# A two-block transformer kernel: the opening in another order, the bias on ScalarE's DMA queue, the compression woven into a slab, normalising ahead of splits, and high parts first in the stages behind a norm

## The reference

```python
def first_block(x, ...):
    for i in range(2):
        hn = rms_norm(x, norm_mix[i])
        x = x + (even_mixer if i == 0 else odd_mixer)(hn, ...)
        x = x + jnp.square(jax.nn.relu(rms_norm(x, norm_mlp[i]) @ mlp_w1[i])) @ mlp_w2[i]   # 1024 -> 4096 -> 1024
    return rms_norm(x, norm_final)

def even_mixer(hn, w_in, w_out, ...):       # 8 heads in three branches, and 4 heads of differential attention
    q, kc, vc, ks, vs, kw, vw, g, dq, dk, dv = split(hn @ w_in)
    kc = compress_kv(kc, pos_k, w1_k, w2_k)  # 15 blocks of 32 tokens: gelu((block + pos) @ w1) @ w2
    vc = compress_kv(vc, pos_v, w1_v, w2_v)
    gates = sigmoid(g)                       # 3 gates per head, one per branch
    # softmax(q k' / 8 + bias[relative position]) v, for each branch and for the differential heads
    return concat([o_a, o_b]) @ w_out

def odd_mixer(hn, w_in, w_out, bias): ...    # 16 heads, q k v = hn @ w_in

def second_block(x, ...):                    # one layer
    # h @ w_in: a gated linear recurrence behind a short convolution, 16 heads of forgetting attention,
    # two gated projections, w_out, a norm and the residual; then w_up (1024 -> 6144), a short
    # convolution, gelu(gate) * value, w_down, a norm and the residual
```

## Time and profile before

| what | us |
|---|---|
| median of three runs | 1252.53 |
| lowest and highest of them | 1247.95, 1256.39 |
| the profiled execution, a run of its own | 1244.96 |
| its span in the profile | 1243.2 |

### The profile page before, as it was taken

The page is one execution under the profiler, slowest core; times in us unless marked ns, Lnnn a source line. Parts: engine busy times, 40 slices in busy tenths (PEclk is TensorE's granted clock), DMA queues, the critical chain, the costliest instruction groups (busy, mean ns, idle before and its releaser), DMA issues.

```text
span 1243.2 us, 21636 instructions
## 1 busy us (share of the span) xinstructions
PE 1158.9 (93%) x9407; PEld 1116.4 (90%) x9407; DVE 796.4 (64%) x1131; ACT 586.6 (47%) x823; POOL 147.4 (12%) x83
## 2 busy tenths in 40 slices
PE   6799888999999999999999999999977979999997
PEld 5798668999999899999999999999975879999997
DVE  6436546877454665787654788776554677888852
ACT  4146654443334464444433556654344446666531
POOL 3000004000031000400022202400060021110100
PEclk8879889999999999999999999999988998999999
DMA  8934205555555443656555371654951353656550
GB/s 218 221 101 136 69 2 162 177 187 187 188 186 169 136 137 106 200 179 194 181 192 178 121 206 41 197 158 150 318 189 35 103 169 105 201 173 218 177 195 36
DMA packets 198771, 195.71 MB, mean 157 GB/s; under 512 B 9692, under 2 KB 196757, under 8 KB 198677
## 3 DMA queue, kind: packets, MB, share of 16 engines
q1 hardware_dynamic: 194116, 190.72, 49.2%
q10 hardware_dynamic: 4560, 3.62, 1.0%
HBM read 192.86 MB, written 1.46 MB: 156 GB/s over the span
## 4 chain that ended last, share of the span: by engine, by line
PE 77%; DVE 9%; SPq 5%; DMA 3%; POOL 2%; ACT 1%; issue 1%; DVEq 0%; ACTq 0%; POOLq 0%
PE ps_gemm L1561 67%; PE ps_score L1626 2%; PE ps_out L1653 2%; DVE w_lo L1026 2%; PE ps_trans L1638 2%; PE ps_score L1837 2%; DMA f_bias<-cum_scr 2%; DVE prob L1066 1%; SPq L509 1%; PE ps_gemm L1731 1%; POOL f_bias L657 1%; SPq L553 1%; DVE act_lo L1032 1%; DMA raw<-in_w_in 1%; DVE prob L1095 1%
## 5 line engine op out<-in xcount | busy, mean ns | idle before, releaser
L1561 PE MATMUL ps_gemm<-act_hi,w_hi 128*128 128x256 f32 x1640 | 467.3, 285 | 27.0 <-DVE act_lo L1032 21.2
L1561 PE MATMUL ps_gemm<-act_lo,w_hi 128*128 128x256 f32 x1640 | 461.8, 282 | 0.0
L1561 PE MATMUL ps_gemm<-act_hi,w_lo 128*128 128x256 f32 x1640 | 461.5, 281 | 0.0
L1026 DVE TENSOR_TENSOR w_lo<-raw,w_hi 128x2048 fp32r<-128x2048 f32 (+2 forms) x179 | 409.5, 2295 | 69.1 <-ACT w_hi L698 68.7
L698 ACT ACTIVATE w_hi<-raw 128x2048 fp32r<-128x2048 f32 (+2 forms) x179 | 332.7, 1862 | 204.0 <-DMA raw<-in_mlp_w 97.9
L1561 PEld LDWEIGHTS ps_gemm<-act_hi,w_hi 128*128 128x128 f32 x1640 | 311.6, 190 | 35.8 <-issue 30.4
L1561 PEld LDWEIGHTS ps_gemm<-act_lo,w_hi 128*128 128x128 f32 x1640 | 311.6, 190 | 0.3
L1561 PEld LDWEIGHTS ps_gemm<-act_hi,w_lo 128*128 128x128 f32 x1640 | 311.3, 190 | 0.2
L1561 PE MATMUL ps_gemm<-hid_hi,w_hi 128*128 128x256 f32 x512 | 143.1, 280 | 0.0
L1561 PE MATMUL ps_gemm<-hid_hi,w_lo 128*128 128x256 f32 x512 | 143.1, 279 | 0.0
L1561 PE MATMUL ps_gemm<-hid_lo,w_hi 128*128 128x256 f32 x512 | 142.8, 279 | 0.0
(11 more groups left out here) (282 smaller groups left out, 1738.1 us busy)
## 6 DMA issues: line engine op xcount, KB each, us to landing
raw<-in_mlp_w SPq DMA_DIRECT2D x64, 1024.0 KB, 5.4
raw<-in_w_in SPq DMA_DIRECT2D x30, 1024.0 KB, 5.7
raw<-in_w_up SPq DMA_DIRECT2D x24, 1024.0 KB, 5.2
raw<-in_od_w_in SPq DMA_DIRECT2D x12, 1024.0 KB, 5.1
raw<-in_w_down SPq DMA_DIRECT2D x12, 1024.0 KB, 5.2
raw<-in_ev_w_in SPq DMA_DIRECT2D x9, 1024.0 KB, 8.4
raw<-in_w_proj_a SPq DMA_DIRECT2D x8, 640.0 KB, 4.3
raw<-in_ev_w_out SPq DMA_DIRECT2D x4, 1024.0 KB, 5.3
```

The costliest lines, as they stand in the source:

```text
L1026: dve.tensor_tensor(w_lo[:, slot, 0:k, 0:n], raw[:, slot, 0:k, 0:n], w_hi[:, slot, 0:k, 0:n].bitcast(F32), ALU.subtract).then_inc(w_ready, 1)
L1561: ins = pe.matmul(dst, lhs, rhs, start=(first and opens and i == 0 and half == 0 and q == 0), stop=(last and closes and i == len(ks) - 1 a ...
```

## The change

1. **DMA queues in the opening.** The 8 bias loads go from SyncE's queue to ScalarE's, with the wait for `brow_out` ahead of them. SyncE issues `cw1` directly behind the parameter rows, ahead of GATE and SV.
2. **ScalarE's order.** Split of slab 0, split of x, the write of the bias rows to HBM, split of slab 1, the wait, the 8 bias loads, `root(0)`, split of slab 2.
3. **TensorE's and VectorE's order.** The bias rows are made and copied behind the transposes and copies of x. The transposes of the parameter rows and their copies go behind Q0.
4. **Compression woven into SV.** `compress_chunk(k)` issues 8 of the 64 matmuls behind each of SV's 8 chunks. The wait for GATE's result to be moved out is in the first of them.
5. **VectorE in attention.** `normalise(i - 1)` goes ahead of the split of the low part.
6. **High parts first.** The first slab of each of the six stages behind a norm runs its 32 matmuls with x_hi, each chunk behind a wait for `act_hi`, and then its 16 matmuls with x_lo behind waits for `act_lo`.

No arithmetic is added or left out, only the order of the additions changes.

```diff
@@ SyncE @@
+        for i, name in enumerate(("k", "v")):
+            sp.dma_start(cw1[:, i, :, :], ...).then_inc(ld["cw"], 16)
         a_slab(GATE)
         a_slab(SV)
-        sp.wait_ge(brow_out, 16)
-        for a in range(P // 16):
-            sp.dma_start(nb[16 * a:16 * a + 16, :, :], src).then_inc(nb_in, 16)
-        for i, name in enumerate(("k", "v")):
-            sp.dma_start(cw1[:, i, :, :], ...).then_inc(ld["cw"], 16)
@@ ScalarE @@
+        split_hi(0)
+        act.wait_ge(par_ok, 1)
+        split_x(0)
         act.wait_ge(brow_ok, 1)
         act.dma_start(... scr_w ..., brow ...).then_inc(brow_out, 16)
-        split_hi(0)
-        act.wait_ge(par_ok, 1)
-        split_x(0)
-        for s in range(1, AHEAD):
-            split_hi(s)
+        split_hi(1)
+        act.wait_ge(brow_out, 16)
+        for a in range(P // 16):
+            act.dma_start(nb[16 * a:16 * a + 16, :, :], src).then_inc(nb_in, 16)
         root(0)
+        split_hi(2)
@@ VectorE, attention @@
+                if 1 <= i < n + 1:
+                    normalise(i - 1)
                 for part in FILL[p].get(i, ()):
                     if part[0] == "in":
                         in_slab(part[1], part[2] == 0, False)
-                if 1 <= i < n + 1:
-                    normalise(i - 1)
@@ VectorE, opening @@
-        dve.wait_ge(brow_ps, 1)
-        dve.tensor_copy(brow[:, :], ps_o[0:16, 0, 0:REL]).then_inc(brow_ok, 1)
...
         for gi in range(4):
             dve.wait_ge(xt, gi + 1)
             dve.tensor_copy(x[:, 2 * gi:2 * gi + 2, :], pair(gi)).then_inc(emptied[gi % 2], 1)
+        dve.wait_ge(brow_ps, 1)
+        dve.tensor_copy(brow[:, :], ps_o[0:16, 0, 0:REL]).then_inc(brow_ok, 1)
...
         a_slab(KV_CMP)
+        a_slab(Q0)
         dve.wait_ge(par_t, 2)
...
-        for j in range(Q0, DQ0):
+        for j in range(SKW, DQ0):
             a_slab(j)
@@ TensorE, gemm @@
+            order = [(k, half, q) for k in ks for half in halves for q in range(3)]
+            if low_last:
+                order = [(k, half, q) for qs in ((0, 2), (1,)) for k in ks for half in halves for q in qs]
+            for i, (k, half, q) in enumerate(order):
+                if before_chunk is not None and half == 0 and q < 2:
+                    before_chunk(k, q)
...
+                if between is not None and half == len(halves) - 1 and q == 2:
+                    between(k)
...
         def x_in(n):
-            def wait(c):
-                pe.wait_ge(xl, PRE_I[n] * NX + c + 1)
+            def wait(c, low):
+                pe.wait_ge(xl if low else xh, PRE_I[n] * NX + c + 1)
@@ TensorE, opening @@
-        pe.wait_ge(ld["bias"], 32)
-        pe.matmul(ps_o[0:16, 0, 0:REL], btab[:, :], buck[:, :], ...).then_inc(brow_ps, 1)
         pe.wait_ge(ld["x"], 32)
...
+        pe.wait_ge(ld["bias"], 32)
+        pe.matmul(ps_o[0:16, 0, 0:REL], btab[:, :], buck[:, :], ...).then_inc(brow_ps, 1)
...
+        def compress_chunk(k):
+            g = g0 + CMP1_GROUP
+            b = g % 2
+            if k == 0:
+                pe.wait_ge(emptied[b], gwait(g))
+                pe.wait_ge(ld["cw"], 16 * 6)
+                gi = g0 + A_GROUPS[KV_CMP]
+                pe.wait_ge(emptied[gi % 2], out_count(gi))
+            for m in range(4 * (k % 4), 4 * (k % 4) + 4):
+                i = k // 4
+                ins = pe.matmul(ps_g[:, b, ...], cw1[:, i, m, :], cmp2[:, i, :, ...], start=(m == 0), stop=(m == 15))
+            if k == KS - 1:
+                ins.then_inc(cmp_ps, 1)
...
         a_slab(0)
         stat(0)
+        a_slab(1)
+        stat_tok(0)
         pe.wait_ge(ld["par"], 16 * len(PARAMS))
...
-        a_slab(1)
-        stat_tok(0)
-        for j in range(SKW, DQ0):
-            a_slab(j)
-        compress(False)
+        a_slab(SKW)
+        a_slab(GATE)
+        a_slab(SV, between=compress_chunk)
         a_slab(DQ0)
-        compress(True)
+        compress()
```

More of the change, by code:

```diff
@@ L1540, in gemm @@
                     pe.wait_ge(emptied[b], gwait(g))
-            for i, k in enumerate(ks):
-                if before_chunk is not None:
-                    before_chunk(k)
-                if before_pair is not None and k % 2 == 0:
-                    before_pair(k // 2)
-                passes = ((w_hi, x_hi), (w_hi, x_lo), (w_lo, x_hi))
-                for half in range(2):
-                    if m is not None and half:
-                        break
-                    for q, (w, xx) in enumerate(passes):
-                        if tok_major:
-                            lhs = xx[:, kc0 + k, half * P:(half + 1) * P]
-                            rhs = w[:, slot, k, 0:n]
-                            dst = ps_g[:, b, half * NS:half * NS + n]
-                        else:
-                            mm = m or P
-                            lhs = w[:, slot, k, half * P:half * P + mm]
-                            rhs = xx[:, kc0 + k, :]
-                            dst = ps_g[0:mm, b, half * T:(half + 1) * T]
-                        ins = pe.matmul(dst, lhs, rhs, start=(first and opens and i == 0 and half == 0 and q == 0),
-                                        stop=(last and closes and i == len(ks) - 1 and q == 2), skip_group_check=True)
@@ new lines, in gemm @@
+            passes = ((w_hi, x_hi), (w_hi, x_lo), (w_lo, x_hi))
+            halves = range(1 if m is not None else 2)
+            order = [(k, half, q) for k in ks for half in halves for q in range(3)]
[4 more added lines that the diff above has]
+                    before_chunk(k, q)
+                if before_pair is not None and k % 2 == 0 and half == 0 and q == 0:
+                    before_pair(k // 2)
+                w, xx = passes[q]
+                if tok_major:
+                    lhs = xx[:, kc0 + k, half * P:(half + 1) * P]
+                    rhs = w[:, slot, k, 0:n]
+                    dst = ps_g[:, b, half * NS:half * NS + n]
+                else:
+                    mm = m or P
+                    lhs = w[:, slot, k, half * P:half * P + mm]
+                    rhs = xx[:, kc0 + k, :]
+                    dst = ps_g[0:mm, b, half * T:(half + 1) * T]
+                ins = pe.matmul(dst, lhs, rhs, start=(first and opens and i == 0),
+                                stop=(last and closes and i + 1 == len(order)), skip_group_check=True)
+                if between is not None and half == len(halves) - 1 and q == 2:
+                    between(k)
@@ L1783, in mlp @@
             for j in range(16):
-                gemm(s0 + j, g0 + j, act_hi, act_lo, before_chunk=x_in(n) if j == 0 else None)
+                gemm(s0 + j, g0 + j, act_hi, act_lo, before_chunk=x_in(n) if j == 0 else None, low_last=j == 0)
                 if j == 0:
@@ L1798, in m_slab @@
             s, g = st["m_in"].s0 + j, st["m_in"].g0 + j
[L1799 removed]
+            gemm(s, g, act_hi, act_lo, before_chunk=x_in(2) if j == 0 else None, low_last=j == 0, tok_major=j % 3 == 2,
                  ks=range(k0, k1), opens=k0 == 0, closes=k1 == KS)
@@ L1813, in _ @@
         for j in range(5):
-            gemm(s0 + j, g0 + j, act_hi, act_lo, before_chunk=x_in(4) if j == 0 else None)
+            gemm(s0 + j, g0 + j, act_hi, act_lo, before_chunk=x_in(4) if j == 0 else None, low_last=j == 0)
             if j == 0:
@@ L1881, in _ @@
         for j in range(24):
-            gemm(s0 + j, g0 + j, act_hi, act_lo, before_chunk=x_in(6) if j == 0 else None)
+            gemm(s0 + j, g0 + j, act_hi, act_lo, before_chunk=x_in(6) if j == 0 else None, low_last=j == 0)
             if j == 0:
```

33 lines of the change are left out of this document (15 added, 18 removed).

## The result

The changed kernel takes 1242.77 us (median of 5 runs, 1240.8 to 1244.57) where the kernel before, run beside it, takes 1251.14 (1247.95 to 1256.39). The ratio is 0.9935, with a 95% interval of 0.9908 to 0.9961. That is 8.4 us, where the prediction had 18.4. The time lies in its range, near the place of the second rival (1244.1). The two profiled executions lie only 4.2 us apart (1244.96 and 1240.80), because the one before was 6.2 us under its median and the one after 2.0 us. So what follows takes the traces apart and adds up to 4.2, not to 8.4.

What follows compares the result with a forecast made beforehand. The prediction took TensorE as the bound, so only its waits or low-clock time could be won. Opening 4.1, part 5 5.0 and part 6 9.3 summed to 18.4 us, from 1252.5 to 1234.1, range 1222 to 1247.

Steps and rivals of the forecast that it cites:

- second rival: Opening: the woven slab stays at half clock, DQ0 ends at 90.8, a loss of 5.9; 1244.1 us; chance 0.15.
- The working at half clock: Opening, gates out to DQ0's end: SV's 42 matmuls 8.9, compression's 64 13.9, DQ0 7.09, together 29.9 us.
- the sum: Opening's DMA: transfers up to DK0 from 21.3 us add up to 34.4 us, so DK0 lands at 55.7.
- the lag: SyncE in the opening: nine small issues took 8.6 us; expected back partly, so 3.0 of 4.5 us won.
- The even alternation: Opening's DMA: with work in both ScalarE's and SyncE's queues, each moves half, so their times add up.
- GATE's lateness: Opening: GATE lands at about 44, behind `cw1` and beside the bias, hidden with 5 us to spare before 60.9.
- third rival: Opening: ScalarE is held in its bias issues, delaying `root(0)`, splits and gates; up to 1255.3 us; chance 0.05.
- fourth rival: Attention and normed stages: parts 5 and 6 give half, total gain 11.3; 1241.2 us; chance 0.12.
- first rival: Opening: the bias costs the weights nothing, DK0 lands near 41, total gain 30.0; 1222.5 us; chance 0.14.

Runs made afterwards that it cites:

- e6: The changed kernel with 40 unused products of 256 columns added ahead of GATE and 40 ahead of the first compression chunk; 1232.10 us.
- e4: The changed kernel with the eight bias loads issued by SyncE behind SV instead of by ScalarE; 1244.83 us.
- e2: The kernel before with parts 5 and 6 alone, its opening untouched apart from the order of slab 0; 1235.48 us.
- e8: The kernel before with part 6 alone, high parts first in the first slab of each normed stage; 1242.91 us.
- e1: The changed kernel with the compression taken out of SV and run as a block behind it; 1232.85 us.
- e5: e1 with GATE and SV loaded ahead of `cw1`, bias issued by SyncE behind DK0, and GATE's and SV's evictions ahead of DK0's and DQ1's splits; 1219.93 us.
- e7: The changed kernel with each compression product replaced by one of a slab's kind (256 columns), leaving the compression out; 1230.78 us.
- e10b: e5 with the bias issued behind DQ1 and the compression woven between SV's last four and DQ0's first four chunks; 1215.94 us.

## Why the prediction missed

| term | forecast | measured |
|---|---|---|
| part 1, the gates earlier | 3.0 | 0.2 (63.40 to 63.16) |
| part 4, gates out to end of DQ0 | 20.97 to 19.9: 1.1 | 20.97 to 31.0: -10.0 |
| part 5 | 5.0 | 5.7 |
| part 6 | 9.3 | 8.4 |

The measured column is from the two traces and adds up to the 4.2 us between them; the medians say 8.4. By either, the forecast of 18.4 was missed in the opening: it was to win 4.1 and lost 9.8.

**Part 4 is the step that failed**, with one sentence: "I take the first 4 us at half clock, which cost 2, then full clock". I took the full slabs' part in the weave for enough to bring the clock back, as it had in a row of slabs. It did not, in 22.8 us. The working at half clock stood right beside it, 29.9 us from the kernel before's own rows, and came out at 31.0. At full clock the prediction had 17.9 us, and e6 took 12.2 for the weave and 5.9 for DQ0. So the sizes were right and the choice between them wrong. One of the prediction's own signs of being wrong, the clock at 0.5 through the compression, is what the trace shows. The reason for the choice was an analogy between two different mixtures of products, and the trace had a row against it: the compression alone had run 13.88 us without a gap at half clock. That weighed more than I let it. A second row was overlooked. The stretch from 40.00 to 46.50 in the earlier trace rows, taken there for 60 matmuls with short rows at full clock, begins with some 20 products of SKW and ends just where the clock falls in GATE's (46.5, shown above). SV's first products then ran at half clock as well. Short products without a gap had thus taken the clock down already in the kernel before.

**Part 1** had the sum right and the lag wrong. I wrote that nothing is won "if that lag stands behind the last big load again", and that is what happened: nine small issues took from 44.40 to 48.95, behind GATE and SV, and in the issues ahead of them SyncE had been held 17.7 us. The rule of the Trainium skill that I weighed there ("DMA: Bandwidth & Descriptors", "Issuing engines are not separate DMA queues") is borne out by the result: DK0 landed as late from either queue (59.94 and 60.65). The even alternation that I read off did not hold from 18 to 30 us, where the bias had the engines nearly alone; it delayed GATE and SV, and by that opened the 5.4 us gap before GATE. I had called GATE's lateness hidden, and it was: e4, with GATE there 12 us earlier, is no faster. The clock was at half when GATE began, but e4 and e6 show that it falls in GATE's products without that gap too.

**Part 2 and 3** went as written or better: `root(0)` ran at 22.20 instead of 26.77, and ScalarE's eight bias issues took 3.99 us in all, none of them held, so the third rival fell. (That SyncE's queue was full while it was held 13.56 us is the prediction's reading; no row shows what held it.) The gain went into a wait of 4.2 us for the parameter rows, which now stood behind the bias.

**Parts 5 and 6** together are 14.0 in the traces against 14.3. Part 5 is 5.7, just above its upper bound of 5.6, and the waits that it was about fell from 25.5 to 20.4. Part 6 is 8.4 in five pieces: 1.9, 2.0, 2.0, 1.2 and 1.3 (2.2, 2.3, 2.3, 0.8 and 1.7 forecast). That the sum is so near is in part luck: e2 by its medians gives 15.4 for both, e8 6.9 for part 6, and each of these is good to some 4 to 6 us. The fourth rival, that they give half, falls with e2. The first rival, that the bias costs the weights nothing, falls with DK0 at 59.94.

**The second rival** had the mechanism, the place and nearly the price (90.8 for DQ0's end, 94.6 measured; the 3.8 between are 2.8 us of later start and 1.1 more at half clock). I gave it 0.15. That its time of 1244.1, a gain of 8.4, is met by the medians so exactly is luck: it has 5.9 us lost in the opening, and 9.8 were. I had priced that 42 of SV's products fall behind the wait. What I had not seen is that they are also what would fill it and bring the clock back: in e1 SV ran on to 65.7, only 1 us past the gates, and the compression began at full clock. e1 and e6 show that either cure, SV ahead of the wait or a full clock at its end, is worth 10 us.

## What to carry over

Work woven into a slab inherits the slab's wait, and the slab the work's: before interleaving, ask what each half could have done in the gap ahead, and put the weave behind the wait, not around it. Before a long run of small products, look at what the clock will be when it begins. An idle stretch or another run of short products ahead of it (here GATE's) may have brought it down. Then price the run at half clock, unless products like those of the slabs stand between. And where a result hangs on a transfer only by the order of an engine's queue (here the gates on DQ0 and DK0, by ScalarE's and VectorE's splits), moving the transfers and then the evictions was worth 12.9 us on top of the unwoven kernel (e1 to e5).

## What the runs showed of the hardware

- The granted clock depended on which products ran, not only on whether TensorE ran. Blocks of 45-column products took it from full to half 3.4 to 4.4 us (e1) and 4 to 5 us (e5) in, without a gap, and GATE's 24-column products did so 4 us in (before, e4) and some 3 us in (e6). Mixed with products of 256 columns, 32 to 42 (64 rows to 42 in the trace), the compression's kept a full clock (12.2 us in e6, 12.4 in e10b) but did not bring back a lost one (22.8 us in the changed kernel). Products of 256 columns alone did, 5 us in in e7 and 4 to 5 us in in e1's SV. The Trainium skill, "TensorE: Matmul & The Clock Gate", section "What's actually happening", ties the clock to how busy TensorE has recently been. The changed kernel's row (22.80 us busy of 22.80, clock 0.50) doesn't go with that in its plain reading, and the measurement decides.
- One core's two DMA queues did not share evenly for long: from 18 to 30 us ScalarE's queue moved 1.44 MB of bias packets and SyncE's 0.11 MB, 129 GB/s together, although SyncE had a 1 MB load issued from 21.71 on. From 894 to 900 us in the kernel before they shared evenly (1.05 and 1.03 MB). What makes the difference, no run shows.
